# A transposed copy of x, scaled by GpSimd, in place of TensorE's transposes of the normed tokens

## The chip, the cores and the metric

The kernel runs on the eight cores of one Trainium2 chip. All cores run the same program on their own part of the data: four sequences, each cut into two halves of 4096 tokens. The metric is the device time of the slowest core in microseconds. The engines are called as in the profile: PE is TensorE's matmul, PEld its weight load, DVE is VectorE, ACT is ScalarE, POOL is GpSimd and SP is SyncE, which here issues all DMAs.

## What is computed

One layer of a hybrid decoder. Shapes: x is (4, 8192, 1024) in float32; the input projection has 2816 columns.

```python
h = rmsnorm(x, norm_g)                       # per token: x * rsqrt(mean(x*x) + 1e-6) * g
proj = h @ w_in                              # att q,k,v,gate (512,128,128,512), ret q,k,v,gate (256,256,512,512)
a = sliding_window_attention(aq, ak, av, sinks) * silu(az)   # window 128, 8 heads, 2 kv heads
r = retention(rq, rk, rv, gn_g) * silu(rz)   # 4 heads, chunks of 128, a state carried over chunks
x = x + concat(a, r) @ w_out
out = rmsnorm(x, final_g)
```

The factor of the RMS norm is one number for each token, and norm_g is folded into the weights.

## The kernel before

**Tiling and staging.** A chunk is 128 tokens, one per partition. Each core handles 32 prefix chunks (the half before its own; only the retention keys are projected, and the retention state is built from them) and then 32 main chunks, which yield output. NP and NM are both 32. The loop of `build_program` runs over steps t; in one step each stage named in `order` is emitted for chunk t minus its offset, so the stages of one chunk are spread over several steps. In the main part `load` of x runs 4 steps ahead (9 for the first seven), `front` 3 ahead, `T` 2 ahead, `P` and `P2` 1 ahead; `R`, `SC` and `scT` are at 0, `PV`, `OR`, `KV` and `M` at 1, `O` at 2.

**Stages at issue.** `st_load` (L492 for the DMA) brings a chunk of x, 512 KB, into one of NX=7 slots `xs`, where it stays until `st_O` adds it to the output. `st_front` computes the token factor: ACT squares and sums (L667), DVE adds the epsilon (L670), POOL raises to the power -0.5 (L673). The same stage scales the rows of x by that factor into `hh` in bf16, on ACT (L519) or DVE (L521). `st_T` transposes `hh` on PE in eight pieces of 128x128 into a PSUM bank (L684), and ACT (L505) or DVE (L507) copies the bank into `hT`, of which there are two, used by turns. `st_P_main` projects `hT` (L691, L697), `st_M` transposes the gated branch outputs `mix` (L1000), `st_PV`, `st_OR` and `st_KV` are the attention and retention matmuls (L887, L973, L977, L912), and `st_O` is the output projection (L1011), the residual sum (L1015), the final norm (L1020, L1022, L1025, L1027) and the store of the output, issued in the same stage.

**PSUM.** Eight banks stand in two rings. Ring A has the four banks 0, 1, 2 and 7 and serves `T`, `P`, the two row norms of q and k, `P2`, `R`, `M` and `O`; the allocations go round in the order of emission, so a bank comes free only when the fourth allocation before has been read out. In one main step ring A is asked thirteen times: O, O, R, the four of P and the norm of q, the two gates of P2 and the norm of k, M, T. Ring B serves the others.

**What sets the order of the work.** `Sched` records all operations with their reads and writes, gives each a cost from a table, and lays them out greedily in time (`schedule`). PE and SP keep the order of emission. ACT, DVE and POOL take operations from a window of 64, by planned start in bins of 0.5 us and then by urgency, which is handed back from the order of PE. Operations with several possible engines (PSUM copies: ACT or DVE) go where they end first by the plan. Each engine's order is then fixed, and each operation waits on semaphores for what it depends on. SP is one queue: a DMA that waits holds all that are behind it. A DMA is planned to land by a bandwidth of 310 GB/s plus 1 us.

**Weights.** They come through three staging slots `wstage` in float32 and are cast to bf16 on arrival (L582, L579, L580, L608); w_out comes in the last six prefix steps and the first two main steps.

Of the kernel before, what the change touches and what calls it, by code (L numbers as in the profile page):

```python
# [10 lines left out]
F32 = mybir.dt.float32  # L11
# [12 lines left out]
NEG = -30000.0  # L24
ATT_SCALE = 64 ** -0.5
SCHEDULE = True
DEFAULT_OPTS = dict(
    pools={"A": [0, 1, 2, 7], "B": [3, 4, 5, 6]},
    order=[("load", -9, -4), ("tload", -3, -4), ("GF", 2, None), ("PV", None, 1),
           ("OR", None, 1), ("KV", None, 1), ("O", None, 2), ("G", 1, None), ("R", None, 0), ("SC", None, 0),  # L30
           ("T", -2, None), ("P", -1, -1), ("scT", None, 0), ("P2", -1, -1), ("M", None, 1), ("T", None, -2),
           ("GT", 1, None), ("front", -4, -3)],
    window=64,
    urgency=True,
    bin_us=0.5,
# [46 lines left out]
class Sched:  # L82
# [127 lines left out]
    def schedule(self, window=40, lat=0.2, dma_lat=4.5, urgency=True, bin_us=0.5, bias=None, bias_pre=None):  # L210
# [37 lines left out]
        while remaining:  # L248
# [96 lines left out]
def build_program(NP, NM, opts=None):  # L345
# [102 lines left out]
    tmpa, b_tmpa = slots("tmpa", 1, [128, 512], F32)  # L448
# [12 lines left out]

    Gbf, GT = yy[0][:].bitcast(BF16), yy[1][:].bitcast(BF16)
    b_Gbf, b_GT = b_yy
    stat2, b_stat2 = slots("stat2", 2, [128, 4], F32)

    ps_all = es.enter_context(nc.psum_tensor("ps", [128, 8 * 512], F32))
# [15 lines left out]
        rr[pool] += 2  # L482
        return ps_all[:, i * 512:(i + 2) * 512], [b_bank[i], b_bank[i + 1]]

    qnames = ["pe", "act", "dve", "pool", "const", "constB", "cs0", "cs1", "dkt"]
# [141 lines left out]
    def is_main(c):  # L627
        return c >= NP

    def st_load(c):  # L630
        sx = c % NX
# [31 lines left out]
        S.add("sp", dma(dst, src), writes=[b_tb[tbx(c)]], dmaq=f"tl{tbx(c)}")  # L663

    def st_front(c):
        sx, st = c % NX, c % 4
        S.add("act", lambda e: e.activation(out=junk[:], in_=xs[sx][:], func=AF.Square,  # L667
                                            accum_out=stat[st][:, 0:1]),
              reads=[b_xs[sx]], writes=[b_junk, b_stat[st]])
        S.add("dve", lambda e: e.tensor_scalar(out=stat[st][:, 1:2], in0=stat[st][:, 0:1], scalar1=1.0 / D,  # L670
                                               scalar2=RMS_EPS, op0=ALU.mult, op1=ALU.add),
              reads=[b_stat[st]], writes=[b_stat[st]])
        S.add("pool", lambda e: e.tensor_tensor(out=stat[st][:, 2:3], in0=stat[st][:, 1:2],  # L673
                                                in1=neghalf[:, 0:1], op=ALU.pow),
              reads=[b_stat[st], b_misc], writes=[b_stat[st]])
        S.add(scale_rows(hh[hx(c)][:], xs[sx][:], stat[st][:, 2:3], D,
                         engines=(opts["hscale_main"] if is_main(c) else opts["hscale_pre"])),
              reads=[b_xs[sx], b_stat[st]], writes=[b_hh[hx(c)]])

    def st_T(c):  # L680
        bank, bb = alloc("A")
        pb = bank.bitcast(BF16)
        for kb in range(8):
            S.add("pe", lambda e, kb=kb: e.transpose(pb[:, kb * 128:(kb + 1) * 128],  # L684
                                                     hh[hx(c)][:, kb * 128:(kb + 1) * 128], ident_bf[:]),
                  reads=[b_hh[hx(c)], b_const], writes=[bb])
        S.add(cp(hT[c % 2][:], pb[:, 0:1024]), reads=[bb], writes=[b_hT[c % 2]])
# [315 lines left out]
        S.add(cp(mixT[s2][:], pb[:, 0:1024]), reads=[bb], writes=[b_mixT[s2]])  # L1003

    def st_O(c):
        s2, sx = c % 2, c % NX
        m = c - NP
        for half in range(2):
            bank, bb = alloc("A")
            for kb in range(8):  # L1010
# [16 lines left out]
        S.add("dve", lambda e: e.scalar_tensor_tensor(out=yy[s2][:], in0=yy[s2][:], scalar=st[:, 2:3], in1=fg_rep[:],  # L1027
                                                      op0=ALU.mult, op1=ALU.mult),
              reads=[b_yy[s2], b_stat2[s2], b_constB], writes=[b_yy[s2]])
        S.add("sp", dma(out_d[m * CH:(m + 1) * CH, :], yy[s2][:]), reads=[b_yy[s2]], dmaq=f"st{s2}")  # L1030

    def run_stage(name, c):
# [5 lines left out]
        if name == "load":  # L1038
            st_load(c)
        elif name == "front":  # L1040
            st_front(c)
        elif name == "T":
            st_T(c)
        elif name == "P":
            if main:
                st_P_main(c, 1)
            else:
                st_P_prefix(c)
        elif name == "P2":
            if main:  # L1050
                st_P_main(c, 2)
        elif name == "tload":
            st_tload(c)
        elif name == "G":
            st_G(c)
        elif name == "GT":
            if c == NP - 1:
                st_GT(c)
        elif name == "GF":
            if c == NP - 1:  # L1060
                st_GF(c)
        elif not main:
            return
        elif name == "KV":
            st_KV(c)
        elif name == "R":
            st_R(c)
        elif name == "SC":
            st_SC(c)
        elif name == "scT":  # L1070
            st_scT(c)
        elif name == "PV":
            st_PV(c)
        elif name == "OR":
            st_OR(c)
        elif name == "M":
            st_M(c)
        elif name == "O":
            st_O(c)

    order = opts["order"]
    t_first = min(o for n, o, m in order if o is not None)
    for t in range(t_first, NT + 3):
        if t == t_first:
            load_wk(0)
            load_wk(1)
# [7 lines left out]
        for task in w_tasks.get(t, ()):  # L1094
            task()
        for name, off_pre, off in order:
            if name == "G":
                for c in range(max(0, t - 3), NP):
                    if t == min(c + 3, NP):
                        run_stage(name, c)  # L1100
                continue
            if off_pre is not None and 0 <= t - off_pre < NP:
                run_stage(name, t - off_pre)
            if name == "load":
                for c in range(NP, NT):
                    if t == c + (off_pre if c - NX < NP else off):
                        run_stage(name, c)
            elif off is not None and t - off >= NP:
                run_stage(name, t - off)

    if SCHEDULE:
# [80 lines left out]
def _core_inputs(xb, first_half, NP, NM, pos_main0, shared):  # L1192
# [45 lines left out]
```

How the kernel before makes its waits and increments, by code:

```python
            def body(e, stream=stream, eng=eng):  # L328
                waited = {}
                for op in stream:
                    for d in op.deps:
                        if waited.get(d.queue, 0) < d.val:
                            e.wait_ge(sems[d.queue], d.val)
                            waited[d.queue] = d.val
                    ins = op.fn(e)
                    if op.signals:
                        ins.then_inc(sems[op.queue], op.inc)
                if eng == "sp":
                    for q in final_waits:
                        if self.totals.get(q, 0) > 0:
                            e.wait_ge(sems[q], self.totals[q])
```

## Time and profile before

| | us |
|---|---|
| time, median of 3 runs (lowest to highest) | 709.88 (709.41 to 710.18) |
| the profiled execution, its own time | 710.5 |
| its span on the slowest core, core 0 | 709.0 |
| spans of the eight cores | 705.6 to 709.0 |
| PE busy in the span | 625.7 (88%) |
| DVE busy | 567.1 (80%) |
| ACT busy | 435.4 (61%) |
| POOL busy | 196.2 (28%) |
| DMA, mean over the span | 110 GB/s |

The span is the time from the first to the last instruction of a core. Matmuls are pipelined and each record includes the time through the array, so records of PE overlap; the distance between two starts tells what a matmul costs, and the record's own length does not. The granted clock is a share of full speed (2.4 GHz).

### The profile page before, as it was taken

What the parts mean: (1) busy time and instruction counts of PE and PEld (TensorE: products, weight loads), DVE (VectorE), ACT (ScalarE), POOL (GpSimd) and SP (SyncE); (2) the same over time, 40 slices, a digit from 0 to 9 for tenths busy, and PEclk for the clock granted to TensorE, in tenths of its full rate; (3) what the DMA queues carried; (4) which work ended last, traced back from release to release, by engine and by line L of the source; (5) the groups of instructions that cost most, each with busy time, mean ns of one, the idle gap of its engine ahead of it and who ended that gap; (6) DMA issues with size and microseconds to landing.
All of it is one profiled execution on the core that took longest, in us unless ns stands there. A gap on an engine that the chain in (4) does not pass through costs nothing.

```text
span 709.0 us, 17169 instructions; the slowest of 8 cores (705.6 to 709.0 us)
## 1 busy us (share of the span) xinstructions
PE 625.7 (88%) x5480; PEld 394.1 (56%) x5555; DVE 567.1 (80%) x1201; ACT 435.4 (61%) x767; POOL 196.2 (28%) x253
## 2 busy tenths in 40 slices
PE   0597786988999999999999999999999999999983
PEld 0464564555665565665655655656556655656641
DVE  0787787446888888888888888878889788888895
ACT  3777667644666666556665566666666666666652
POOL 3634242101222222222232222232222222322231
PEclk9998899999999999999999999999999999999998
DMA  7999979600112312202232131221203221200002
GB/s 234 320 334 328 300 210 321 218 16 1 61 45 89 108 33 98 93 3 99 83 118 75 38 114 67 85 76 49 101 32 120 76 76 63 89 31 31 31 32 89
DMA packets 23847, 77.76 MB, mean 110 GB/s; under 512 B 3152, under 2 KB 3536, under 8 KB 23760
## 3 DMA queue, kind: packets, MB, share of 16 engines
q1 hardware_dynamic: 23760, 76.67, 32.2%
q8 instruction: 47, 0.77, 0.5%
q14 instruction: 40, 0.33, 0.2%
HBM read 59.88 MB, written 16.78 MB: 108 GB/s over the span
## 4 chain that ended last, share of the span: by engine, by line
PE 76%; DVE 8%; issue 6%; DMA 4%; ACT 3%; POOL 1%; DVEq 0%; SPq 0%; POOLq 0%; ACTq 0%
PE ps L691 33%; PE ps L1011 14%; PE ps L697 10%; PE ps L684 4%; PE ps L854 3%; PE ps L931 3%; PE ps L887 2%; DMA wstage<-w_r 2%; PE ps L1000 2%; DVE gate L817 1%; DMA wstage<-w_o 1%; POOL stat L673 1%; PE ps L873 1%; PE ps L741 1%; PE ps L977 1%
## 5 line engine op out<-in xcount | busy, mean ns | idle before, releaser
L691 PE MATMUL ps<-Wa,hT 128*128 128x512 bf16 (+2 forms) x1000 | 168.1, 318 | 10.1 <-ACT hT L505 4.6
L691 PEld LDWEIGHTS ps<-Wa,hT 128*128 128x128 bf16 x1032 | 90.1, 101 | 66.7 <-issue 9.0
L1011 PE MATMUL ps<-Wo,mixT 128*128 128x512 bf16 x481 | 109.0, 379 | 11.5 <-DVE den L894 8.1
L691 PE MATMUL ps<-Wb,hT 128*128 128x512 bf16 x512 | 115.7, 379 | 0.0
L863 POOL TENSOR_SCALAR_AFFINE_SELECT PT<-PT 128x1024 bf16<-128x1024 bf16 x63 | 75.6, 1201 | 126.1 <-ACT PT L857 124.3
L987 POOL TENSOR_TENSOR gns<-gns,neghalf 128x4 f32<-128x4 f32 x32 | 33.7, 1052 | 205.3 <-DVE stat L670 114.4
L1011 PEld LDWEIGHTS ps<-Wo,mixT 128*128 128x128 bf16 x512 | 48.4, 98 | 65.1 <-issue 11.9
L691 PEld LDWEIGHTS ps<-Wb,hT 128*128 128x128 bf16 x512 | 48.8, 98 | 53.1
L857 ACT ACTIVATE PT<-ps,negC 128x1024 bf16<-128x1024 f32 x64 | 70.9, 1111 | 0.7 <-PE ps L697 0.2
L667 ACT ACTIVATE junk<-xs 128x1024 bf16<-128x1024 f32 x64 | 67.1, 1048 | 4.7 <-DMA xs<-x_all 3.4
L697 PEld LDWEIGHTS ps<-hT,Wb 128*128 128x128 bf16 x1024 | 61.2, 99 | 7.2 <-issue 0.7
L673 POOL TENSOR_TENSOR stat<-stat,neghalf 128x1 f32<-128x1 f32 x64 | 37.2, 590 | 96.5 <-DVE stat L670 95.4
L697 PE MATMUL ps<-hT,Wb 128*128 128x128 bf16 x1024 | 63.9, 222 | 0.0
L814 ACT ACTIVATE gate<-ps 128x512 f32<-128x512 f32 x64 | 38.0, 594 | 39.1 <-PE ps L1000 21.5
L505 ACT ACTIVATE kT<-ps 128x256 bf16<-128x256 bf16 x31 | 11.9, 383 | 80.8 <-PE ps L832 80.7
L817 DVE SCALAR_TENSOR_TENSOR gate<-gate,ps 128x512 f32<-128x512 f32 x64 | 43.6, 682 | 8.5 <-ACT gate L814 6.7
L684 PE MATMUL ps<-ident_bf_s,hh 128*128 128x128 bf16 x320 | 26.0, 228 | 26.3 <-DVE stat L670 19.2
L1027 DVE SCALAR_TENSOR_TENSOR yy<-yy,stat,fg_rep_s 128x1024 f32<-128x1024 f32 x32 | 44.5, 1392 | 3.8 <-POOL stat L1025 3.5
L505 ACT ACTIVATE hT<-ps 128x1024 bf16<-128x1024 bf16 x37 | 37.7, 1019 | 15.8 <-PE ps L684 6.7
L1015 DVE TENSOR_TENSOR yy<-ps,xs 128x512 f32<-128x512 f32 x64 | 44.1, 690 | 3.2 <-PE ps L1011 0.3
L723 DVE TENSOR_TENSOR rotu<-ps,tb 128x512 f32<-128x512 f32 x48 | 33.0, 688 | 10.7 <-PE ps L691 9.4
L854 PE MATMUL ps<-aqT,kTa 128*128 128x512 bf16 x127 | 34.2, 379 | 6.0 <-DVE Sst L920 4.6
(126 smaller groups left out, 1135.6 us busy)
## 6 DMA issues: line engine op xcount, KB each, us to landing
xs<-x_all SPq DMA_DIRECT2D x64, 512.0 KB, 8.4
out<-yy SPq DMA_DIRECT2D x32, 512.0 KB, 3.0
wstage<-w_r SPq DMA_DIRECT2D x16, 640.0 KB, 11.3
tb<-tabs SPq DMA_DIRECT2D x32, 256.0 KB, 4.4
wstage<-w_o SPq DMA_DIRECT2D x8, 512.0 KB, 8.5
wstage<-w_k SPq DMA_DIRECT2D x2, 512.0 KB, 6.7
gate<-cs_pre SPq DMA_DIRECT2D x2, 512.0 KB, 12.4
fg_rep_s<-fg_rep SPq DMA_DIRECT2D x1, 512.0 KB, 7.9
```

The lines of the kernel that those rows point to most:

```text
L505: d[en] = lambda e: e.activation(out=out, in_=in_, func=AF.Copy)
L667: S.add("act", lambda e: e.activation(out=junk[:], in_=xs[sx][:], func=AF.Square, accum_out=stat[st][:, 0:1]), reads=[b_xs[sx]], writes=[b ...
L673: S.add("pool", lambda e: e.tensor_tensor(out=stat[st][:, 2:3], in0=stat[st][:, 1:2], in1=neghalf[:, 0:1], op=ALU.pow), reads=[b_stat[st], ...
L684: S.add("pe", lambda e, kb=kb: e.transpose(pb[:, kb * 128:(kb + 1) * 128], hh[hx(c)][:, kb * 128:(kb + 1) * 128], ident_bf[:]), reads=[b_h ...
L691: S.add("pe", lambda e, kb=kb: e.matmul(bank[:, c0:c0 + n], lhsT=hT[c % 2][:, kb * 128:(kb + 1) * 128], rhs=W[:, kb, w0:w0 + n], start=(kb ...
L697: S.add("pe", lambda e, kb=kb: e.matmul(bank[:, c0:c0 + 128], lhsT=W[:, kb, w0:w0 + 128], rhs=hT[c % 2][:, kb * 128:(kb + 1) * 128], start ...
L817: S.add("dve", lambda e, bank=bank, gi=gi: e.scalar_tensor_tensor(out=gate[s2][:, gi * 512:(gi + 1) * 512], in0=gate[s2][:, gi * 512:(gi + ...
L854: S.add("pe", lambda e, bank=bank, sk=sk, g=g, first=first: e.matmul(bank[:, g * 512:(g + 1) * 512], lhsT=kTa[sk][g][:], rhs=aqT[s2][:], s ...
L857: S.add("act", lambda e, blk=blk, bank=bank: e.activation(out=PT[s2][blk][:], in_=bank, func=AF.Exp, bias=negC[s2][:, 0:1], scale=ATT_SCAL ...
L863: S.add("pool", lambda e, blk=blk, sgn=sgn, op=op: e.affine_select(out=PT[s2][blk][:], in_=PT[s2][blk][:], pattern=[[0, 8], [-sgn, 128]], ...
L1011: S.add("pe", lambda e, kb=kb, bank=bank, half=half: e.matmul(bank[:, 0:512], lhsT=mixT[s2][:, kb * 128:(kb + 1) * 128], rhs=Wo[:, kb, hal ...
L1027: S.add("dve", lambda e: e.scalar_tensor_tensor(out=yy[s2][:], in0=yy[s2][:], scalar=st[:, 2:3], in1=fg_rep[:], op0=ALU.mult, op1=ALU.mult ...
```

## The change

Seven edits go together.

1. The host also passes x of the main part transposed (`x_t`: for each chunk, partition = position within a block of 128 model columns, eight blocks of 128 tokens side by side). A stage `xload` brings it, 512 KB per chunk, into a `wstage` slot, 3 steps ahead.
2. The token factor, one number on each partition, must stand in a row for this layout. A stage `rw` writes the 128 numbers of a chunk to a scratch row in DRAM (4 steps ahead), and `rr` reads the row back into all 128 partitions (`rrow`, 64 KB, 3 steps ahead). Both are DMAs of SP.
3. `st_T` of a main chunk is now one POOL instruction, 128x1024, float32 times float32 into bf16 `hT`, 2 steps ahead as before. The eight transposes, their bank of ring A, the copy of the bank and the scaling into `hh` are gone for main chunks. Prefix chunks are as before.
4. `front` of main chunks runs 5 steps ahead, not 3, and has six slots for the factor. The x that it reads is loaded 7 steps ahead; the first five main chunks go through the two `yy` buffers, much earlier, with steps listed in `early`.
5. x for the residual sum is loaded a second time (`xres`), one step before `O`. All loads into `xs` share one ring of seven.
6. The store is a stage of its own, one step later than `O`.
7. The planner takes a row DMA to land 14 us after issue, and hands urgency on between SP's DMAs less strictly.

```diff
-    order=[("load", -9, -4), ("tload", -3, -4), ("GF", 2, None), ("PV", None, 1),
+    order=[("rr", None, -3), ("rw", None, -4), ("load", -9, -7), ("tload", -3, -4), ("xload", None, -3), ("store", None, 3),
+           ("xres", None, 1), ("GF", 2, None), ("PV", None, 1),
...
-           ("GT", 1, None), ("front", -4, -3)],
+           ("GT", 1, None), ("front", -4, -5)],
...
             for d in o.deps:
-                if o.urg < d.urg:
-                    d.urg = o.urg
+                u = o.urg + 250 if o.eng == "sp" and d.eng == "sp" else o.urg
+                if u < d.urg:
+                    d.urg = u
...
+                if op.queue[0:2] in ("rw", "rr"):
+                    op.t1 = st + 14.0
...
+    def st_load(c, res=False):
+        if is_main(c) and not res and c < NP + 5:
+            m = c - NP
+            x_slot[(c, res)] = NX + m % 2
+            S.add("sp", dma(yy[m % 2][:], x_d[c * CH:(c + 1) * CH, :]), writes=[b_yy[m % 2]], dmaq=f"xe{m % 2}")
+            return
+        sx = x_rr[0] % NX
+        x_rr[0] += 1
+        x_slot[(c, res)] = sx
...
+        if is_main(c):
+            return
+        S.add(scale_rows(hh[hx(c)][:], xt[:], stat_[:, 2:3], D, engines=opts["hscale_pre"]),
+              reads=[b_xt, b_st], writes=[b_hh[hx(c)]])
...
+    def st_rw(c):
+        m = c - NP
+        S.add("sp", dma(rs_d[m:m + 1, :].rearrange("o p -> p o"), statm[c % 6][:, 2:3]), reads=[b_statm[c % 6]],
+              writes=[b_rs[m % 4]], dmaq=f"rw{m % 2}")
+
+    def st_rr(c):
+        m = c - NP
+        S.add("sp", dma(rrow[m % 3][:], rs_d[m:m + 1, :].to_broadcast([128, CH])), reads=[b_rs[m % 4]],
+              writes=[b_rrow[m % 3]], dmaq=f"rr{m % 3}")
+
+    def st_xload(c):
+        m = c - NP
+        st_t, b_st, q = stage_slot()
+        xT_slot[c] = (st_t, b_st)
+        S.add("sp", dma(st_t[:, 0:D], xT_d[m * CH:(m + 1) * CH, :]), writes=[b_st], dmaq=q)
 
     def st_T(c):
+        if is_main(c):
+            st_t, b_st = xT_slot[c]
+            m = c - NP
+            i0 = st_t[:, 0:D].rearrange("p (k t) -> p k t", k=8)
+            o = hT[c % 2][:].rearrange("p (k t) -> p k t", k=8)
+            i1 = rrow[m % 3][:].unsqueeze(1).to_broadcast([128, 8, CH])
+            S.add({e: (lambda e: e.tensor_tensor(out=o, in0=i0, in1=i1, op=ALU.mult)) for e in T_ENG},
+                  reads=[b_st, b_rrow[m % 3]], writes=[b_hT[c % 2]], cost={"pool": 2.3, "dve": 1.25})
+            return
...
+    early = dict(load=(-15, -13, -8, -6, -4, 99), front=(-12, -10, -6, -4, -2, 99), rw=(-8, -6, -3, -1, 0, 99),
+                 rr=(-3, -2, 99, 99, 99, 99))
...
+            if name in early:
+                for c in range(NP, NT):
+                    m = c - NP
+                    if t == max(t_first + 4, min(c + off, NP + early[name][min(m, 5)])):
+                        run_stage(name, c)
+                off = None
...
+    d["x_t"] = np.ascontiguousarray(main.reshape(NM, CH, 8, 128).transpose(0, 3, 2, 1)).reshape(NM * CH, D)
```

## Rows read from the trace of the kernel before

**Rows 1.** The windows view: us, busy (x) of PE PEld DVE ACT POOL, clock, DMA share, GB/s.

```profile
120.00:130.00 10.00, 5.64 (x61) 4.46 (x63) 4.65 (x12) 3.91 (x7) 3.05 (x4) 0.83 1.01 330
184.00:690.00 506.00, 484.03 (x4363) 299.97 (x4419) 435.47 (x929) 319.69 (x582) 136.22 (x146) 1.00 0.20 71
```

**Rows 2.** The chain that ended last, in order of time: start, microseconds, what.

```profile
127.18 2.45 PE ps L697 x40
...
178.70 3.40 PE ps L1011 x15
...
403.87 3.40 PE ps L1011 x15
...
418.54 0.69 DVE gate L817
...
420.76 0.68 DVE gate L817
...
421.80 3.40 PE ps L1011 x15
...
664.39 3.38 PE ps L1011 x15
...
680.66 3.40 PE ps L1011 x15
```

**Rows 3.** The waits of PE, 184 to 690: microseconds, times, longest.

```profile
PE ps L1011 <- DVE den L894: 8.1, 11, 1.3
PE ps L684 <- DVE gate L817: 3.9, 6, 1.0
```

**Rows 4.** The timeline of PE around one transposed chunk.

```profile
419.37 0.61 PE L684 MATMUL ps<-ident_bf_s,hh 128*128 128x128 bf16 x8 [0.48 <-DVE gate L817]
419.81 0.65 PE L887 MATMUL ps<-Vaug,PT 128*128 128x65 bf16 x16
```

**Rows 5.** Groups of instructions, 184 to 690: count, busy, mean ns, idle before.

```profile
L684 PE MATMUL ps<-ident_bf_s,hh 128*128 128x128 bf16 x224 | 17.0, 219 | 4.6 <-DVE gate L817 3.9
...
L519 ACT ACTIVATE hh<-xs,stat 128x1024 bf16<-128x1024 f32 x14 | 16.1, 1148 | 7.6 <-POOL stat L673 7.6
...
L521 DVE TENSOR_SCALAR hh<-xs,stat 128x1024 bf16<-128x1024 f32 x13 | 12.6, 972 | 1.2 <-POOL stat L673 1.2
...
L507 DVE CAST kTa<-ps 64x128 bf16<-64x128 f32 x41 | 11.7, 287 | 6.9 <-PE ps L691 5.5
```

**Rows 6.** The tile view of hT, 184 to 690: min/median/max ns.

```profile
L505 ACT ACTIVATE hT<-ps x21: 1012/1023/1032, 194.5 to 663.8; 128x1024 bf16<-128x1024 bf16 x21
L507 DVE COPY hT<-ps x7: 680/692/693, 211.8 to 629.1; 128x1024 bf16<-128x1024 bf16 x7
```

**Rows 7.** POOL's operations nearest to the new one: min/median/max ns.

```profile
L649 POOL TENSOR_TENSOR tb<-gate,dkt x32: 608/615/1324, 16.7 to 102.3; 128x256 f32<-128x256 f32 x32
...
L580 POOL CAST Wo<-wstage x3: 1036/1036/1430, 115.1 to 125.8; 128x1024 bf16<-128x1024 f32 x3
```

**Rows 8.** POOL's timeline over one step.

```profile
401.58 0.55 POOL L1025 TENSOR_TENSOR stat<-stat,neghalf 128x1 f32<-128x1 f32 x1 [4.17 <-DVE stat L1022]
410.60 1.01 POOL L987 TENSOR_TENSOR gns<-gns,neghalf 128x4 f32<-128x4 f32 x1 [8.47 <-DVE stat L670]
```

**Rows 9.** One collision of DVE and POOL, and DVE's spread, 184 to 690.

```profile
274.82 1.36 DVE L512 TENSOR_TENSOR qk<-rotu,rotw 128x256 bf16<-128x256 f32 x1
...
274.81 1.09 POOL L863 TENSOR_SCALAR_AFFINE_SELECT PT<-PT 128x1024 bf16<-128x1024 bf16 x1 [0.46 <-ACT PT L857]
...
L512 DVE TENSOR_TENSOR qk<-rotu,rotw x29: 408/418/1361, 192.1 to 677.4; 128x256 bf16<-128x256 f32 x29
...
L1027 DVE SCALAR_TENSOR_TENSOR yy<-yy,stat,fg_rep_s x29: 1273/1278/2114, 189.0 to 671.4; 128x1024 f32<-128x1024 f32 x29
```

**Rows 10.** DMA issues, 90 to 180: count, KB each, median microseconds to landing.

```profile
wstage<-w_o SPq DMA_DIRECT2D x8, 512.0 KB, 8.5
```

**Rows 11.** The wait of PE at the change from prefix to main part.

```profile
PE ps L748 <- ACT sqk L754: 4.6, 1, 4.6
```

More of the change, by code:

```diff
@@ L286, in schedule @@
                 free_at[e] = st + op.cost[e]
+                if op.queue[0:2] in ("rw", "rr"):
+                    op.t1 = st + 14.0
+                    remaining -= 1
+                    continue
                 dma_free = max(st + 1.0, dma_free) + op.cost["dma"]
@@ L357, in build_program @@
     dk_d = dram("dk_pre", [128, NP * 4], F32)
+    xT_d = dram("x_t", [NM * CH, D], F32)
+    rs_d = nc.dram_tensor("rs_scr", [NM, CH], F32, kind="Internal").ap()
     tab_d = dram("tabs", [NM * CH, 512], F32)
@@ L447, in build_program @@
     den, b_den = slots("den", 2, [128, 16], F32)
-    tmpa, b_tmpa = slots("tmpa", 1, [128, 512], F32)
     gns, b_gns = slots("gns", 2, [128, 12], F32)
@@ L463, in build_program @@
     b_Gbf, b_GT = b_yy
+    rrow, b_rrow = slots("rrow", 3, [128, CH], F32)
+    b_rs = [Buf(f"c_rs{i}") for i in range(4)]
+    statm, b_statm = slots("statm", 6, [128, 4], F32)
     stat2, b_stat2 = slots("stat2", 2, [128, 4], F32)
@@ L483, in alloc_pair @@
         return ps_all[:, i * 512:(i + 2) * 512], [b_bank[i], b_bank[i + 1]]
-    qnames = ["pe", "act", "dve", "pool", "const", "constB", "cs0", "cs1", "dkt"]
+    qnames = ["pe", "act", "dve", "pool", "const", "constB", "cs0", "cs1", "dkt", "rw0", "rw1", "rr0", "rr1", "rr2", "xe0", "xe1"]
     qnames += [f"ws{i}" for i in range(NST)]
@@ L628, in is_main @@
         return c >= NP
-    def st_load(c):
-        sx = c % NX
+    x_slot, x_rr = {}, [0]
+    def st_load(c, res=False):
[7 more added lines that the diff above has]
+        x_slot[(c, res)] = sx
         S.add("sp", dma(xs[sx][:], x_d[c * CH:(c + 1) * CH, :]), writes=[b_xs[sx]], dmaq=f"xl{sx}")
@@ L665, in st_front @@
     def st_front(c):
[L666 to L670, printed above, removed]
+        sx = x_slot[(c, False)]
+        xt, b_xt = ((xs + yy)[sx], (b_xs + b_yy)[sx])
+        stat_, b_st = (statm[c % 6], b_statm[c % 6]) if is_main(c) else (stat[c % 4], b_stat[c % 4])
@@ L671, in st_front @@
+        S.add("act", lambda e: e.activation(out=junk[:], in_=xt[:], func=AF.Square,
+                                            accum_out=stat_[:, 0:1]),
+              reads=[b_xt], writes=[b_junk, b_st])
+        S.add("dve", lambda e: e.tensor_scalar(out=stat_[:, 1:2], in0=stat_[:, 0:1], scalar1=1.0 / D,
                                                scalar2=RMS_EPS, op0=ALU.mult, op1=ALU.add),
-              reads=[b_stat[st]], writes=[b_stat[st]])
-        S.add("pool", lambda e: e.tensor_tensor(out=stat[st][:, 2:3], in0=stat[st][:, 1:2],
+              reads=[b_st], writes=[b_st])
@@ L674, in st_front @@
+        S.add("pool", lambda e: e.tensor_tensor(out=stat_[:, 2:3], in0=stat_[:, 1:2],
                                                 in1=neghalf[:, 0:1], op=ALU.pow),
[L675 to L678, printed above, removed]
-    def st_T(c):
+              reads=[b_st, b_misc], writes=[b_st])
@@ L1005, in st_O @@
     def st_O(c):
-        s2, sx = c % 2, c % NX
-        m = c - NP
+        s2, sx = c % 2, x_slot[(c, True)]
         for half in range(2):
@@ L1029, in st_O, with st_store @@
               reads=[b_yy[s2], b_stat2[s2], b_constB], writes=[b_yy[s2]])
+    def st_store(c):
+        s2, m = c % 2, c - NP
         S.add("sp", dma(out_d[m * CH:(m + 1) * CH, :], yy[s2][:]), reads=[b_yy[s2]], dmaq=f"st{s2}")
@@ L1041, in run_stage @@
             st_front(c)
+        elif name == "xload":
+            if main:
+                st_xload(c)
+        elif name in ("rw", "rr"):
+            if main:
+                (st_rw if name == "rw" else st_rr)(c)
+        elif name == "xres":
+            if main:
+                st_load(c, True)
         elif name == "T":
@@ L1079, in run_stage @@
             st_O(c)
+        elif name == "store":
+            st_store(c)
     order = opts["order"]
+    early = dict(load=(-15, -13, -8, -6, -4, 99), front=(-12, -10, -6, -4, -2, 99), rw=(-8, -6, -3, -1, 0, 99),
+                 rr=(-3, -2, 99, 99, 99, 99))
     t_first = min(o for n, o, m in order if o is not None)
-    for t in range(t_first, NT + 3):
+    for t in range(t_first, NT + 5):
         if t == t_first:
@@ L1103, in build_program @@
                 run_stage(name, t - off_pre)
[L1104 to L1108, printed above, removed]
+            if off is not None and t - off >= NP:
                 run_stage(name, t - off)
```

2 lines of the change are left out of this document (added).

## The prediction

> **What bounds the kernel now.** I read the windows first, stretch by stretch. From 184 to 690 us, the steady main part, PE is busy for 484 of 506 us at the full granted clock, DMA at 0.20 of its engines, DVE for 435 us, ACT for 320 and POOL for 136 [rows 1]. PE sets the pace and DVE is the only other engine near it. Next the chain of waits, for the distance between equal points. L1011 (the output projection) opens each main step. It stands at 178.70 and at 664.39 with 28 steps between: 485.7 / 28 = 17.35 us a step. The steps are not equal: 403.87 to 421.80 takes 17.93. The step from 664.39 to 680.66 takes 16.27 [rows 2], and it is the first whose chunk needs no transpose of x, since the chunks have run out. So the trace already holds one sample of a step without T. Third, the waits of PE in this stretch: 8.1 us before L1011 in 11 pieces and 3.9 us before L684 in 6 [rows 3] are the two large ones. The rest of the difference between the mean and 16.27 is the transposes.
>
> What stands behind the 8.1 us? In the chain, L1011 at 421.80 follows DVE's gate product L817 at 420.76 [rows 2]. L1011 asks for a bank of ring A; four allocations back is the second gate of P2, which L817 reads out. Those in between are the norm of k, M and T. T is itself one of the thirteen users of the ring. L684 waits for the first gate's bank in the same way [rows 3].
>
> Ahead of the steady part DMA is the limit: from 120 to 130 us its engines are busy all the time at 330 GB/s, PE for 5.6 of 10 us, with the clock at 0.83 [rows 1]. PE's longest wait there, 4.6 us, is for ACT, which held a cast of w_out in front [rows 11].
>
> **The transposes.** The eight go from 419.37 to 419.81 [rows 4], 0.44 us of PE. There are 28 groups of eight in the stretch (224 instructions [rows 5]) and nothing hides them, as PE is the pace. 28 x 0.44 = 12.3 us off. Four more main chunks have their T before 184 us, partly where PE waits anyway: 0.9 us off of at most 1.8.
>
> **The stalls of the ring.** With twelve allocations in a step, the first L1011 takes the bank of the first gate and the second L1011 that of the second gate, 1.7 us later. The 3.9 us before L684 go with the instruction. Of the 8.1 us before L1011 I let 2 stand, for what is late next: the copy of M's bank into mixT, which starts when M's transposes end and on DVE is as long as hT's copy, 0.69 [rows 6]. That is 10.0 us off in all. From both sides: 3.9 us if L1011 finds another late partner, 12.0 if both go, and the whole of 28 x (17.35 - 16.27) - 12.3 = 17.9 us if every step becomes like the sample.
>
> **DVE and ACT.** DVE loses 12.6 us of scaling and 7 copies of 0.69 [rows 5, 6]: 17.4 us, 0.62 a step. ACT loses 16.1 and 21 copies of 1.02: 37.6 us, 1.34 a step. By itself this is worth nothing, as neither is the pace; it is slack for the next paragraph. The planner can also move PSUM copies such as kTa (11.7 us on DVE [rows 5]) over to ACT, which I don't count.
>
> **The new POOL instruction.** The trace has none of its size. From below, the cast of 128x1024 with one input takes 1.04 us; from above, four times the two-input product of 128x256 is 4 x 0.608 = 2.43 us [rows 7]; with DVE in the way once, its longest two-input instruction of 1.27 more [rows 9]. I take 2.3, since the two-input row is of the same kind. POOL was busy 136 us and gets 28 x 2.3 = 64 more: capacity is no question. Place matters. hT has two buffers and the chunk is needed only a step later, and POOL sits idle for 8.47 us before 410.60 [rows 8], so the instruction fits there and PE doesn't wait for it. In front of an `affine_select` or a power it would delay these by up to 2.3 us.
>
> The cost is on DVE. At 274.82 a DVE product of two SBUF tiles takes 1.36 us while its median is 0.418, and POOL's `affine_select` began at 274.81 and took 1.09; the last norm L1027, also with two SBUF inputs, ranges from 1.27 to 2.11 [rows 9]. So a DVE instruction of this kind stands still until POOL's is over: 0.94 of 1.09 us here. The new one is twice as long and comes in each step, so DVE loses from 0 (POOL meets only PSUM readers) to 2.3 us a step. I take 1.0, as the collision is not certain and on the average sets in midway. DVE then stands at 14.93 - 0.62 + 1.0 = 15.3 us a step (14.93 is 435.47 by 506 / 17.35 steps [rows 1, 2]), more than before in a shorter step, 15.3 of 16.6. This delays bank read-outs now and then: 4 us given back over the 28 steps, with ends 0 and, if DVE becomes the pace, the rival below.
>
> The Trainium skill, SBUF — State Buffer, section "Who interferes with whom", says that a VectorE instruction with two SBUF inputs and a GpSimd instruction that reads SBUF exclude one another for the whole length, whichever came first. The trace agrees (0.94 of 1.09 us), and the rule speaks against this change; what it would give if every new instruction cost DVE its full length is the second rival.
>
> **DMAs and waits.** Per steady step x comes twice (512 KB more), the row is written and read (64 KB in SBUF): at 0.20 of the DMA engines before [rows 1] this is covered, at a cost of 0. `rr` waits on SP for the landing of `rw`; behind it stand loads that are 4 to 7 steps ahead, xload 3 ahead, the store and xres. A step of 16.6 us lies between `rw` and `rr`, and even in the crowded stretch 512 KB took 8.5 us to land [rows 10]. The store waits for L1027 a step later than before and so holds SP less. xres has a step of time. Cost 0; if the cover is gone, each microsecond that SP loses shifts xload, which still has most of a step.
>
> **The passage from prefix to main.** Here the cover is thin. Two chunks of transposed x must land before the second main projection, 1.05 MB at 330 GB/s = 3.2 us in a stretch where DMA is the pace [rows 1], and their `wstage` slots are shared with w_out, so some loads of w_out wait for T. Rows of 4 bytes a partition go into the same crowded engines. I take 4 us; the ends are -1 (the early x lands in a better place and the 4.6 us wait [rows 11] shrinks) and +17, when T of the first chunk waits for a row and a transposed x one after the other, two landings of 8.5 us [rows 10].
>
> **The sum**, from the profiled execution's 710.5 us (span 709.0, 1.5 around it): 710.5 - 12.3 - 0.9 - 10.0 + 4 + 4 = 695.3. The median of the runs is 0.6 below the profiled one, so 694.7; I say 695. Its own range is 689 to 702.
>
> **Rivals.**
> *All stalls go.* Twelve allocations on four banks give each user the same partner in each step, the sample's 16.27 becomes the rule, and DVE keeps up. 28 x 1.08 = 30.2 off, 0.9 off, 4 on for the passage: 683.4, less 0.6, 683. For it: the sample, and ACT's slack. Against it: the sample's DVE has little else to do. 0.14.
>
> *POOL holds DVE for its whole length* (the other side: slower). Place: DVE's two-input instructions L1027, gate, mix, Sst and qk; price: 2.3 us a step. DVE then needs 14.93 - 0.62 + 2.3 = 16.6 us busy, and of the 2.42 us a step in which it is not busy now (17.35 - 14.93) I let half stay: 17.8 us a step, 0.45 more than now, x 28 = +12.6. With +4 for the passage 727, less 0.6: 726. It turns the change to a loss from a block of about 1.7 us a step on (14.31 + 1.7 + 1.2 = 17.2, and the passage). For it: the collisions above. Against it: DVE has PSUM readers to do in between, and one block of the full length needs POOL to start just before such an instruction. 0.12.
>
> *The passage eats it.* The +17 in place of +4: 708. For it: DMA at 1.01 of its engines and ACT casts that hold others up [rows 1, 11]. Against it: the first row is written five prefix steps before it is read. 0.14.
>
> *That the transposes leave but PE doesn't speed up* would need a partner of L1011 that is late by the same 0.44; it lies in the main case's upper end.
>
> **Numbers.** Main case 0.60, all stalls go 0.14, DVE held 0.12, passage 0.14. A change of under 0.2% (1.4 us) can't be told from none here. Faster by more: 0.60 + 0.14 and a third of the passage case, 0.78; within: 0.05; slower: 0.12 and a third of the passage case, 0.17. The range that holds 8 in 10 goes from the stall-free case to above the passage case, 683 to 712; left out are DVE held (0.12) and the edges.
>
> **What would show it.** Right: no L684 after about 125 us; L1011 to L1011 at 16.5 to 16.8; the wait before L1011 under 3 us in all; the new POOL instruction at about 2.3 us in the former idle time, and L1027 or the gate product longer where it overlaps; DVE's busy share near 0.92. Wrong: steps over 17.2 with waits for DVE spread over all users of ring A (DVE held); the first L697 of a main chunk later than 140 us (it was at 127.2 [rows 2]), with PE waiting for POOL's write of hT (the passage); waits for hT in the steady part, which would say that rows or transposed x are late and that SP's queue is not covered.

## The result, and the profile after

The changed kernel takes 1011.82 us (median of 4 runs, 1008.84 to 1015.28) against 710.03 us beside it: a ratio of 1.425, 95% interval 1.421 to 1.428. The forecast was 695, range 683 to 712. The time lies 300 us above the upper end, and most of that comes from a part that the forecast had priced at nothing. In all that follows, ratios, and the times of e7, e14, e16 and e17, leave out executions in which one half of the chip ran longer at a lower clock; e2 and e12 had no others and e4 only one (872.96 us), so for these three all times are given.

In the profiled execution core 1 is the slowest, with a span of 1007.3 us; cores 4 and 5 needed 866 and 845 us, the six others about 1000.

First the head of the page after, then its windows (columns as in [rows 1]): the steady stretch, and two pieces of one main step.

```profile
span 1007.3 us, 19452 instructions; the slowest of 8 cores (845.1 to 1007.3 us)
...
PE 694.9 (69%) x5299; PEld 415.0 (41%) x5299; DVE 583.7 (58%) x1193; ACT 396.8 (39%) x712; POOL 270.6 (27%) x284
...
q1 hardware_dynamic: 42192, 112.34, 74.7%
...
184.00:690.00 506.00, 362.36 (x2779) 214.04 (x2780) 291.01 (x594) 187.04 (x350) 128.98 (x109) 0.84 0.76 90
576.00:592.00 16.00, 13.73 (x89) 6.86 (x88) 11.98 (x25) 5.86 (x12) 2.19 (x3) 0.89 0.76 31
592.00:598.00 6.00, 2.04 (x34) 1.77 (x31) 0.00 (x0) 0.82 (x3) 0.00 (x0) 1.00 0.83 293
```

In the stretch from 184 to 690 us PE was busy for 484 of 506 us before [rows 1] and is busy for 362 now; its granted clock is 0.84 in place of 1.00, so what PE still does is slower too. DMA's engines are busy at 0.76 in place of 0.20, and yet move only 90 GB/s. Both together say that the engines are held for long by few bytes. From 576 to 592 us the engines are busy at 0.76 and move 31 GB/s; right after, from 592 to 598, they move 293 GB/s at 0.83.

What was issued before the slow piece stands in the timeline of SP (start, us, what):

```profile
574.62 0.33 SPq L503 DMA_DIRECT2D rs_scr<-statm  x1
575.04 0.37 SPq L503 DMA_DIRECT2D xs<-x_all  x1
575.61 0.33 SPq L503 DMA_DIRECT2D tb<-tabs  x1
576.03 0.38 SPq L503 DMA_DIRECT2D wstage<-x_t  x1
576.50 0.38 SPq L503 DMA_DIRECT2D out<-yy  x1
577.04 4.91 SPq L503 DMA_DIRECT2D xs<-x_all  x1
582.87 0.33 SPq L503 DMA_DIRECT2D rrow<-rs_scr  x1
```

The first is the write of 128 factors of 4 bytes. What is behind it hardly moves for some 16 us and then lands nearly at once. The last load of x, for the residual sum, is issued at 577.04; it is the longest piece of this step in the chain of waits (start, us, what), and the waits of DVE and SP over the whole span (us, times, longest) show how the step then closes on itself:

```profile
577.04 22.74 DMA xs<-x_all
...
DVE yy L1064 <- DMA xs<-x_all: 140.2, 19, 14.4
...
SPq L340 <- POOL statm L695: 311.1, 21, 23.7
SPq L340 <- DMA rs_scr<-statm: 164.7, 18, 21.2
```

DVE's residual sum waits 140 us for x, where L1015 had no such wait. This delays PE and through it POOL, whose product T waits for hT; the next factor comes behind that in POOL's queue, and SP's next write waits for the factor, 311 us in all. SP also waits 165 us for writes to land before it may read the row. The first L1060 (the output projection, L1011 before) stands at 233.4 us, 54.7 later than before [rows 2], and 31 steps further on the last is 762.4 us later against 521.0: 24.6 us a step in place of 16.8, the short steps of the end included.

### The profile page after: what moved, and what is told of

Its sections match the earlier page's. It is cut to its first block, busy times and chain, and to the rows that moved or that the text cites. A ratio compares the mean times of both kernels' runs of the same rounds, so it can differ in the third digit from the quotient of the medians.

```text
span 1007.3 us, 19452 instructions; the slowest of 8 cores (845.1 to 1007.3 us)
## 1 busy us (share of the span) xinstructions
PE 694.9 (69%) x5299; PEld 415.0 (41%) x5299; DVE 583.7 (58%) x1193; ACT 396.8 (39%) x712; POOL 270.6 (27%) x284
## 3 DMA queue, kind: packets, MB, share of 16 engines
q1 hardware_dynamic: 42192, 112.34, 74.7%
## 4 chain that ended last, share of the span: by engine, by line
DMA 40%; PE 32%; issue 11%; DVE 7%; POOL 3%; SPq 3%; ACT 2%; another core or an unknown queue 1%; POOLq 1%; DVEq 0%; ACTq 0%
DMA xs<-x_all 25%; PE ps L741 14%; PE ps L747 6%; PE ps L1060 5%; DMA wstage<-w_o 4%; DMA wstage<-x_t 4%; DMA rs_scr<-statm 3%; SPq L503 3%; DMA wstage<-w_r 2%; PE ps L904 2%; POOL hT L728 2%; DMA dkt<-dk_pre 1%; ACT junk L689 1%; DVE yy L1064 1%; PE ps L937 1%
## 5 line engine op out<-in xcount | busy, mean ns | idle before, releaser
L741 PE MATMUL ps<-Wa,hT 128*128 128x512 bf16 (+2 forms) x1032 | 188.3, 343 | 13.0 <-DVE hT L518 6.6
L728 POOL TENSOR_TENSOR hT<-wstage,rrow 128x1024 bf16<-128x1024 f32 x32 | 75.8, 2370 | 449.9 <-PE ps L741 131.9
L1060 PE MATMUL ps<-Wo,mixT 128*128 128x512 bf16 x512 | 123.7, 395 | 19.3 <-issue 4.4
L741 PE MATMUL ps<-Wb,hT 128*128 128x512 bf16 x512 | 123.8, 396 | 15.5 <-issue 5.7
L741 PEld LDWEIGHTS ps<-Wa,hT 128*128 128x128 bf16 x1032 | 98.5, 109 | 81.0 <-issue 30.1
L747 PE MATMUL ps<-hT,Wb 128*128 128x128 bf16 x1024 | 81.6, 250 | 18.4 <-issue 11.5
L747 PEld LDWEIGHTS ps<-hT,Wb 128*128 128x128 bf16 x1024 | 77.3, 115 | 27.9 <-issue 23.2
L1060 PEld LDWEIGHTS ps<-Wo,mixT 128*128 128x128 bf16 x512 | 49.3, 101 | 85.7 <-issue 38.0
L1076 DVE SCALAR_TENSOR_TENSOR yy<-yy,stat,fg_rep_s 128x1024 f32<-128x1024 f32 x32 | 45.5, 1423 | 37.9 <-POOL stat L1074 37.5
L689 ACT ACTIVATE junk<-xs 128x1024 bf16<-128x1024 f32 x59 | 62.2, 1054 | 13.0 <-DMA xs<-x_all 11.5
L1069 ACT ACTIVATE junk<-yy 128x1024 bf16<-128x1024 f32 x32 | 33.8, 1055 | 68.9 <-DVE tmpc L813 40.9
L747 PE MATMUL ps<-hT,Wa 128*128 128x128 bf16 x264 | 24.7, 248 | 52.4 <-DVE yy L1064 31.5
L904 PEld LDWEIGHTS ps<-aqT,kTa 128*128 128x128 bf16 x128 | 11.1, 99 | 108.4 <-issue 103.4
L516 ACT ACTIVATE kT<-ps 128x256 bf16<-128x256 bf16 x32 | 12.3, 384 | 107.1 <-PE ps L882 73.1
## 6 DMA issues: line engine op xcount, KB each, us to landing
yy<-x_all SPq DMA_DIRECT2D x5, 512.0 KB, 11.5
rrow<-rs_scr SPq DMA_DIRECT2D x32, 64.0 KB, 16.8
```

The costliest lines, as they stand in the source:

```text
L689: S.add("act", lambda e: e.activation(out=junk[:], in_=xt[:], func=AF.Square, accum_out=stat_[:, 0:1]), reads=[b_xt], writes=[b_junk, b_st])
L728: S.add({e: (lambda e: e.tensor_tensor(out=o, in0=i0, in1=i1, op=ALU.mult)) for e in T_ENG}, reads=[b_st, b_rrow[m % 3]], writes=[b_hT[c % ...
L741: S.add("pe", lambda e, kb=kb: e.matmul(bank[:, c0:c0 + n], lhsT=hT[c % 2][:, kb * 128:(kb + 1) * 128], rhs=W[:, kb, w0:w0 + n], start=(kb ...
L747: S.add("pe", lambda e, kb=kb: e.matmul(bank[:, c0:c0 + 128], lhsT=W[:, kb, w0:w0 + 128], rhs=hT[c % 2][:, kb * 128:(kb + 1) * 128], start ...
L904: S.add("pe", lambda e, bank=bank, sk=sk, g=g, first=first: e.matmul(bank[:, g * 512:(g + 1) * 512], lhsT=kTa[sk][g][:], rhs=aqT[s2][:], s ...
L1060: S.add("pe", lambda e, kb=kb, bank=bank, half=half: e.matmul(bank[:, 0:512], lhsT=mixT[s2][:, kb * 128:(kb + 1) * 128], rhs=Wo[:, kb, hal ...
```

## Experiments

The runs are grouped by what they tell apart.

### The write, the read, neither

```diff
 def st_rw(c):                                   # e1, e3: the write left out
-    S.add("sp", dma(rs_d[m:m + 1, :].rearrange("o p -> p o"), statm[c % 6][:, 2:3]), ...)
+    return
 def st_rr(c):                                   # e1: a constant row; e2, e3: no read, rrow set to 1
-    S.add("sp", dma(rrow[m % 3][:], rs_d[m:m + 1, :].to_broadcast([128, CH])), ...)
+    S.add("sp", dma(rrow[m % 3][:], fg_d[m:m + 1, 0:CH].to_broadcast([128, CH])), ...)
```

> The changed kernel without the write of the token factors to DRAM; the row is read (128 x 512 bytes, the same source row for all partitions) from a constant input with values near 1 in its place, so the factors are left out of the result. Theory W (each 4-byte piece of the write holds a DMA engine for about 1.6 us: the excess of DMA time over the bytes is some 6700 engine-us, 210 per chunk, for 128 pieces; 8 pieces per engine = 13 us a step in which nothing behind it moves): the time falls to 690 to 720 us and the DMA share of the steady part to about 0.35. Theory R (the read of one DRAM row by 128 partitions is what is slow): stays at 950 or more. Theory C (neither is slow in itself; the wait of SP for the write's landing holds all loads): 690 to 730, with a DMA share as low as under W.

Measured: 724.51 us, ratio 1.019 (1.015 to 1.022). First L1060 (here L1059) at 184.6, then 529.6 us to the last. From 184 to 690 us the DMA engines are busy at 0.37 (0.76 with the write). The time is 4 us above the range that W had.

> The changed kernel with the write of the factors but without the read of the row (rrow is set once to 1, so the factors are left out of the result): SP no longer waits for the write. W: 850 to 1000 us, DMA share still over 0.6, steps of 22 us or more, since each step's write blocks the loads behind it for 13 us or so. R: 690 to 720. C: 690 to 730.

Measured: 1044.38 us (1040.35 to 1046.04). SP's DMAs take 0.703 of the engines' time. Without the read, and so without SP's wait for the write's landing, nothing is won; the time is even above W's range.

> Neither write nor read of the row; all the rest of the change stays (x transposed and x a second time, POOL's product of 2.35 us, DVE's collisions, the early loads of the passage). All three theories: the time of the change without its row, 690 to 705 us, which is the prediction's main case (695). Over 710 would mean that the rest of the change costs as well (POOL holding DVE, or the passage).

Measured: 711.28 us, ratio 1.0002 (0.999 to 1.001). So the write is the loss (W holds in kind, R and C fall with e2), but the rest of the change gains nothing either: the upper end of what was expected is passed.

### The write by itself

```diff
 # e4, on the kernel before, with ("rw", None, -2) ahead of "load"
+    S.add("sp", dma(rs_d[m:m + 1, :].rearrange("o p -> p o"), stat[c % 4][:, 2:3]), ...)
 # e7: rs_d has 128 rows of 512 bytes a chunk, a piece goes to each
+    S.add("sp", lambda e: e.dma_start(out=rs_d[m * CH:(m + 1) * CH, 0:1], in_=stat[c % 4][:, 2:3], ...), ...)
 # e8: 512 bytes a piece, from a constant tile
+    S.add("sp", dma(rs_d[m * CH:(m + 1) * CH, :], causal[:, 0:CH]), ...)
 # e12: e4 from ACT's queue
+    S.add("act", dma(rs_d[m:m + 1, :].rearrange("o p -> p o"), stat[c % 4][:, 2:3]), ...)
```

> The kernel before with only the write of each main chunk's factors added (32 writes of 128 x 4 bytes, nobody reads them). W: each write holds the loads and stores behind it for 13 us or so in a step of 17.4; the kernel before has its loads 3 to 4 steps ahead, so the time rises by 10 to 150 us, and the DMA share of the steady part from 0.20 to over 0.6. R and C: 710 to 715 us, DMA share 0.20 to 0.25.

Measured: 895.23 us (872.96 to 905.07). 32 writes of half a kilobyte, which nobody reads, cost the kernel before (711.39 beside it) 162 to 194 us, 184 by the medians: more than W had let them cost.

> The kernel before with one write of 128 x 4 bytes per main chunk, as in the run with the write alone (895 us), but each 4-byte piece to a DRAM row of its own, 512 bytes apart. Theory L (the pieces are slow because they fall into one 512-byte line of DRAM, one after the other): 709 to 720 us. Theory S (a 4-byte piece is slow wherever it goes): 850 to 920.

Measured: 717.89 us (a single execution), against 710.41 beside it.

> The kernel before with one write of 128 x 512 bytes per main chunk (64 KB of a constant tile, next to each other in DRAM; what is written is not the factors). L and S: 709 to 714 us, as full pieces in their own lines are like the output store in small. Theory N (it is the number of pieces, 128 per write): 850 to 920, as with 4 bytes.

Measured: 713.36 us, ratio 1.004 (1.003 to 1.005).

> The kernel before with the write of 128 x 4 bytes into one 512-byte row per main chunk, issued from ACT's queue and not SP's. Theory L1 (the pieces hold the DMA engines themselves, whichever queue they come from): 850 to 920 us as from SP. Theory L2 (only the ring of SP is held up, and SP's own wait for the factor adds to it): 712 to 730 us.

Measured: 883.34 us (877.60 to 887.76). For the slowest core the other queue is no remedy. It isn't without effect: the quickest core of each execution needs 747 to 758 us here and 787 to 846 in e4. Why is open.

The queue lines of the pages (packets, MB, share of 16 engines' span) of before, e4 (the write in one line), e7 (spread), and e12 (from ACT's queue, two lines):

```profile
q1 hardware_dynamic: 23760, 76.67, 32.2%
...
q1 hardware_dynamic: 28368, 76.68, 59.5%
...
q1 hardware_dynamic: 28368, 76.68, 35.4%
...
q1 hardware_dynamic: 23760, 76.67, 48.3%
...
q10 hardware_dynamic: 4608, 0.02, 0.5%
```

Both writes add 4608 packets (4096 pieces, and 512 others) and 0.02 MB. From the shares, (0.595 x 871.4 - 0.322 x 709.0) x 16 / 4096 = 1.13 us of an engine for each piece in one line, and (0.354 x 716.4 - 0.322 x 709.0) x 16 / 4096 = 0.10 us for each that has a line of its own. From ACT's queue the pieces' own packets take 0.5%, and those of SP's queue grow from 32.2% of 709.0 us to 48.3% of 878.2, 228 to 424 us of 16 engines: what waits is the traffic beside them. So it is not the 4 bytes, nor the count, nor SP's queue, but that the 128 pieces lie next to each other in 512 bytes of DRAM. Only distances of 4 and of 512 bytes were run; how far apart is enough, and whether it takes pieces from several DMA engines, is not shown.

The Trainium skill, DMA: Bandwidth & Descriptors, section "Specifications", states 512 bytes as the smallest transfer for full rate, with a read-modify-write below it. By that, pieces of 4 bytes would be slow wherever they go; the spread write at 717.9 us against 895 shows that here this is at most the small part.

### The same in the changed kernel, and the read

```diff
 # e17: rs_d with a row for each piece; the row is read from a constant
-    S.add("sp", dma(rs_d[m:m + 1, :].rearrange("o p -> p o"), statm[c % 6][:, 2:3]), ...)
+    S.add("sp", lambda e: e.dma_start(out=rs_d[m * CH:(m + 1) * CH, 0:1], in_=statm[c % 6][:, 2:3], ...), ...)
 # e16: e1 with 128 different rows read
-    dma(rrow[m % 3][:], fg_d[m:m + 1, 0:CH].to_broadcast([128, CH]))
+    dma(rrow[m % 3][:], fg_d[:, 0:CH])
```

> The changed kernel with its write of 128 x 4 bytes, but each piece to a DRAM row of its own, 512 bytes apart, and the row read from a constant row in place of the one written (the factors are left out of the result). Theory L (one line of DRAM is the loss): 724 to 745 us, the 724.5 without any write and the 7 us that the spread write cost the kernel before, or some more, as the SP queue waits for the write. If the write costs the changed kernel by the wait of SP for the factor or by its pieces wherever they go: over 800.

Measured: ratio 1.018 (1.016 to 1.021), 721.85 to 723.05 us: no more than e1 without any write. The time from issue to landing of the write (slowest core, us) in the changed kernel, and then in e17:

```profile
DMA to landing us min/median/max: 8.4/16.8/21.6
...
DMA to landing us min/median/max: 1.4/1.7/8.4
```

The pieces' adjacent addresses are the whole of the step from some 724 to 1012 us, and SP's waits are their consequence. (e17 also reads another row; but e2, which reads none, kept the loss.)

> The changed kernel without the write, with the read of 64 KB from 128 different rows of the same constant input (values near 1; the factors are left out of the result). Theory M (many readers of one 512-byte row are slow): 710 to 715 us, as without the read. Theory O (order, bytes and place in the queue): 722 to 727, as with the one row.

Measured: ratio 1.018 (1.015 to 1.021), 721.33 and 723.22 us. M falls: 128 readers of one row cost at most 3 us more than readers of 128 rows. The read costs the changed kernel 10 to 13 us over e3 all the same. Why (its bytes, SP's order, or the order that the planner makes around it) was not settled.

### POOL's product and DVE

```diff
 # e5, on e3: one block of eight, the block goes round; planned cost unchanged
+    kb = (m // 2) % 8
+    o, i0, i1 = hT[c % 2][:, kb * 128:(kb + 1) * 128], st_t[:, kb * 128:(kb + 1) * 128], rrow[m % 3][:]
 # e6, on e3: four pieces
+    for h in range(4):
+        S.add(... e.tensor_tensor(out=o[:, 2 * h:2 * h + 2], in0=i0[:, 2 * h:2 * h + 2], in1=i1[:, 0:2], op=ALU.mult) ...)
```

> The changed kernel with neither write nor read of the row, and POOL's product cut to one of its eight blocks (128x128; the block goes round with the chunk, the other seven keep what they held; the order planned is the same, since the planner's cost of 2.3 us is left). Theory P (the rest of the change gains nothing because POOL's product of 2.35 us holds DVE's two-input instructions, 0.9 us a step by the longer means of gate, mix and Sst): the steps fall from 17.1 to 16.4 to 16.7 us, DVE's busy share to 0.84, the time to 692 to 700 us. Theory Q (something else: the doubled loads, or the order that the planner found): 707 to 712 us, steps still over 17.

Measured: 695.64 us, ratio 0.978 (0.976 to 0.981).

> Neither write nor read of the row, and POOL's product in four pieces of 128x256 one after the other. P: what DVE waits at one meeting is at most 0.6 us in place of 2.35, though it may meet more than one piece: 698 to 706 us. If each meeting costs what POOL has left of the whole product, or if Q holds: 708 to 714.

Measured: 704.15 us, ratio 0.991 (0.989 to 0.993). POOL has more to do than in e3 (busy for 295.5 us against 271.5), so it is not POOL's own time that costs, but what it takes from DVE. P holds. Whether the length of one meeting or the sum counts isn't told apart: DVE's busy time over the span falls too, from 575.7 us in e3 to 562.5 here and 550.5 in e5, about as the time does.

One meeting in e3, POOL's timeline and DVE's:

```profile
214.50 2.35 POOL L728 TENSOR_TENSOR hT<-wstage,rrow 128x1024 bf16<-128x1024 f32 x1 [4.47 <-PE ps L962]
...
214.07 0.68 DVE L867 SCALAR_TENSOR_TENSOR gate<-gate,ps 128x512 f32<-128x512 f32 x1
214.66 3.28 DVE L1076 SCALAR_TENSOR_TENSOR yy<-yy,stat,fg_rep_s 128x1024 f32<-128x1024 f32 x1
217.86 0.15 DVE L944 TENSOR_TENSOR den<-ps,esk 128x8 f32<-128x8 f32 x1
...
220.57 1.19 PE L904 MATMUL ps<-aqT,kTa 128*128 128x512 bf16 x4 [2.33 <-DVE mix L952]
```

The last norm L1076, 1.27 us long when alone, starts 0.16 after POOL's product and takes 3.28. The residual sum, the denominators and the gate product come behind it, and PE waits 2.33 us for the attention output at 220.57. Groups of DVE from 184 to 690 (count | busy, mean ns), before, e3 and e5:

```profile
L512 DVE TENSOR_TENSOR mix<-gg,gns 128x512 bf16<-128x512 f32 x30 | 24.2, 807 | 10.3 <-POOL gns L987 10.2
...
L512 DVE TENSOR_TENSOR gate<-gate,den 128x512 f32<-128x512 f32 x29 | 19.9, 687 | 1.6
...
L512 DVE TENSOR_TENSOR Sst<-Sst,cdtab_s 128x256 f32<-128x256 f32 x30 | 13.2, 440 | 0.0
...
L523 DVE TENSOR_TENSOR gate<-gate,den 128x512 f32<-128x512 f32 x30 | 31.2, 1041 | 2.5
L523 DVE TENSOR_TENSOR mix<-gg,gns 128x512 bf16<-128x512 f32 x30 | 30.6, 1019 | 9.4 <-POOL gns L1037 8.9 <-issue 0.2
...
L523 DVE TENSOR_TENSOR Sst<-Sst,cdtab_s 128x256 f32<-128x256 f32 x30 | 17.8, 595 | 0.0
...
L523 DVE TENSOR_TENSOR mix<-gg,gns 128x512 bf16<-128x512 f32 x31 | 30.3, 979 | 8.9 <-POOL gns L1041 8.6
...
L523 DVE TENSOR_TENSOR gate<-gate,den 128x512 f32<-128x512 f32 x30 | 20.9, 698 | 2.5
...
L523 DVE TENSOR_TENSOR Sst<-Sst,cdtab_s 128x256 f32<-128x256 f32 x30 | 15.8, 527 | 0.1
```

Gate 687 to 1041 ns, mix 807 to 1019, Sst 440 to 595: 0.72 us a step, and with the smaller ones (tmpc +0.13, qk +0.06, L1076 +0.02) 0.93. With an eighth of the product the gate is back at 698 and Sst at 527, but mix only falls to 979: most of mix's growth isn't the size of the product. DVE's whole work in this stretch is 446.6 us in e3 and 433.8 in e5, by their mean steps of 17.1 and 16.6 us 15.1 and 14.3 us a step.

### The row without a DMA

```diff
 # e9 to e15: the row by ACT, PE and ACT
+    S.add("act", lambda e: e.activation(out=diag[m % 2][:], in_=ident_bf[:], func=AF.Copy, scale=statm[c % 6][:, 2:3]), ...)
+    S.add("pe", lambda e: e.matmul(bank[:, 0:128], lhsT=ones_f[:], rhs=diag[m % 2][:], start=True, stop=True), ...)
+    S.add("act", lambda e: e.activation(out=rrow[m % 3][:], in_=bank[:, 0:128], func=AF.Copy), ...)
 # e9, e10, e11: own bank ahead of M; e14: own bank after M; e13, e15: columns 128 to 255 of the bank of k's norm
 # POOL's product: whole in e9 and e15, four pieces in e10, e13 and e14, eight in e11
```

> The whole computation with the row made on chip: ACT scales the unit matrix by the factors (128x128 float32), one float32 matmul of PE with a matrix of ones brings the row into all partitions of a ring A bank, ACT copies it to rrow; no DMA of a row. All else as in the changed kernel, POOL's product whole. Theory P and L together: the run with neither write nor read (711 us) plus about 0.25 us of PE a step and a thirteenth allocation in ring A: 711 to 722 us.

Measured: 743.56 us, ratio 1.046 (1.044 to 1.048).

> The same with POOL's product in four pieces: the run with pieces (704 us) plus 0.25 us a step of PE, 704 to 712 us. If it comes below 708 it beats both kernels and computes everything.

Measured: 760.17 us, ratio 1.068 (1.066 to 1.070).

> The same with eight pieces of 128x128. P: a meeting costs DVE at most 0.33 us, so 1 to 3 us below the four pieces, unless POOL's start-up per instruction makes up for it (POOL has the time).

Measured: 779.47 us, ratio 1.094 (1.092 to 1.097). All three miss what was expected, and more pieces make it worse where they had made it better. In e9 PE waits before M (us, times, longest), from 184 to 700:

```profile
PE ps L1061 <- DVE gate L878: 20.6, 19, 2.0
```

This looked like the place of the new allocation in ring A, so it was moved.

> The whole computation with the row made by PE's float32 matmul, written into the free half of the bank that k's norm takes anyway, so that ring A has twelve allocations a step; POOL's product in four pieces. Theory G (the place in the ring cost the 33 us and more): 704 to 712 us, no wait of M for the gate product. Theory H (the float32 matmul with its two ACT operations costs it by itself): 740 or more, as with a bank of its own ahead of M (743 whole, 760 in pieces).

Measured: 743.56 us, ratio 1.046 (1.044 to 1.048).

> The same, but the row matmul with a bank of its own right after M, in the place of the removed transposes: thirteen allocations in the order of the kernel before. G: 706 to 716 us, above the shared bank, since the first output matmul again waits for the second gate. H: 740 or more.

Measured: ratio 1.058 (1.056 to 1.060), 751.05 to 752.34 us.

> Shared bank as in the first of these runs, with POOL's product whole. G and P (POOL's product holds DVE): 3 to 9 us above the one with pieces, 710 to 719. H: 740 or more.

Measured: 736.91 us, ratio 1.036 (1.035 to 1.038). In e13 and e15 the wait of M for the gate product is gone, and the time is 17 and 7 us below e10 and e9, so the place counts, but most of the loss stays and G falls; e13 and e14 are where H had them. In e15 the first output projection comes at 193.2 us, 11.5 later than in e3, and PE waits for ACT's square of k (e15, 184 to 690):

```profile
PE ps L765 <- ACT sqk L833: 6.9, 10, 1.4
PE ps L1089 <- ACT rrow L728: 3.6, 6, 0.9
```

e3 waited 1.3 us for that square. The two ACT operations cost by what they stand in front of, but they don't account for all of it, and why pieces help without the row (711 to 704) and hurt with it (737 to 744) stays open. No version that computes everything beat the kernel before.

## Why the prediction was wrong, step by step

**The step that failed** is "DMAs and waits", with its "Cost 0". It priced the row by its bytes ("64 KB in SBUF") and asked whether `rw` lands within a step. It did not ask what 128 pieces of 4 bytes cost and what they do to the traffic behind them. Measured in the changed kernel: 287 us between it and e1, and with the pieces spread, nothing. The write took 16.8 us to land by the median and up to 21.6, so the step of 16.6 us between `rw` and `rr` didn't cover it. The cover that I named, loads several steps ahead, held for x, tabs and x_t but for 20 us in all; xres, one step ahead and last in the queue behind the write, had none (140 us). The trace of before held no store of that kind, and a cost without a row has no upper end near zero: the range should have been open above, or the forecast should have said that its range holds only if the write is harmless. The passage paragraph mentions the 4 bytes and gives them no price. The signs of being wrong pointed past it: the first projection of a main chunk starts at 154.2 us after 6.8 us of waiting for hT (the sign of the passage), and the steps are over 17.2 with PE waiting behind DVE (close to the sign of DVE held), while the sign of an uncovered SP queue, PE waiting for hT in the steady part, did not come: that wait is the only one.

**The transposes** (12.3 and 0.9 us): right as far as the steps show. The transposes of `hh` (L734 in the changed kernel) stand only in the prefix, and 21 of the 29 steps of e5 are 16.3 to 16.6 us, as the sample of 16.27 had said; their mean is 16.6, where 16.5 to 16.8 was forecast.

**The stalls of the ring** (10.0 off, 2 left): right in kind, too large in size. In e5 PE waits before the output projection, for whichever partner, 4.8 us in all from 184 to 690, where I let 2 stand, against 8.1 before it and 3.9 before L684 [rows 3]. The three longest entries:

```profile
PE ps L1064 <- ACT mixT L516: 1.5, 2, 1.3
...
PE ps L1064 <- DVE den L951: 1.1, 5, 0.2
...
PE ps L1064 <- DVE tmpc L814: 0.7, 3, 0.2
```

**The POOL instruction** (2.3 us): right; the tile view of hT in the changed kernel (min/median/max ns):

```profile
L728 POOL TENSOR_TENSOR hT<-wstage,rrow x32: 2337/2352/2669, 151.7 to 943.4; 128x1024 bf16<-128x1024 f32 x32
```

**DVE held by POOL**: the mechanism and the size (1.0 us a step forecast, 0.93 measured, DVE's work a step 15.1 against 15.3) were right; the term drawn from them was mis-sized. I let 4 us of it reach PE; e3 less e5 is 15.6. DVE loses its 0.93 us a step not evenly but partly in single blocks of up to 2 us, and behind the one shown above stand the products that PE waits for. What the Trainium skill says in SBUF — State Buffer, section "Who interferes with whom", is borne out at nearly full length: 3.28 us is 1.27 and 2.01 of the 2.19 that POOL's 2.35 had left. The rival that made this a loss was too strong, the main case too weak; the truth of this part alone, 711, lay at the range's upper edge.

**The passage** (4 us): right for e3, whose first output projection is 3.0 us later than before, 181.7 against 178.7; in the changed kernel it is 54.7, again by the write: without it (e1) 5.9.

With every other term as it was, the sum without the row would have read 695; e3 has 711; 11.6 of the 16.6 between them are the give-back. Of the other 5, up to 2.8 are the waits in front of the output projection that I had taken off; the rest was not split further.

## What to carry to other kernels

A column of numbers, one per partition, doesn't become a row cheaply by a write of 4-byte pieces into adjacent DRAM addresses; put the pieces 512 bytes apart (0.10 us of an engine a piece against 1.13) or test it alone in the old kernel before building on it. Reading such spread pieces back as a row was not run. When the DMA share rises much more than GB/s (here 0.20 to 0.76 against 71 to 90), look at the smallest transfer in the queue, not the largest. When a GpSimd instruction goes beside a busy VectorE, what counts is what it takes from VectorE's two-input instructions and which product stands behind them, not GpSimd's own load.

## What the runs showed of the hardware that was not expected

- 32 writes of 128 x 4 bytes, each into 512 adjacent bytes, cost 184 us (895 against 711), or 173 from ACT's queue (883); with 512 bytes between the pieces 7 to 8, with pieces of 512 bytes 3.
- In ACT's queue the pieces' own packets take 0.5% of the engines' time, and the time of the other queue's packets grows from 228 to 424 us of 16 engines.
- 128 partitions reading the same 512 bytes are hardly slower than 128 reading different ones (724.4 and 724.7 against 721.3 and 723.2 us).
- In the changed kernel cores 0 and 1, 2 and 3, 4 and 5, 6 and 7 go together: in each of the six executions on record a pair needs either 987 to 1014 us or 842 to 885, and which pairs are quick changes. From the queue shares of the profiled one (74.7% of 1007.3 us on core 1, 68.8% of 845.1 on core 5, 49.9% of 720.3 in e17) the same pieces take an estimated 1.54 and 0.87 us of an engine. What joins the two cores of a pair was not tested.
